# One stage instead of three: merge, the context's norm and its first queries

## The reference, cut to what matters

```python
merged = (g_a * (y_rw @ w_out_rwkv) + g_b * (y_cv @ w_out_conv) + g_c * (y_at @ w_out_attn))   # gates: sigmoids
x = x + gate1 * (merged @ w_o)
x = x + gate2 * peer_ffn(modulate(x, shift2, scale2), lp)      # modulate: rms_norm(x) * (1 + scale) + shift

# peer_ffn, per token and head (8 heads):
q = hx @ wq                                  # two halves of 64
s = q . sub_keys                             # 2 x 128 scores
sv, si = top_k(s, 16); comb = all 16 x 16 sums; fv, fi = top_k(comb, 16)
idx = e1 * 128 + e2                          # 16 of 16384 experts
out = sum_k softmax(fv)_k * gelu(u[idx_k] . hx) * v[idx_k]
```

## Time and profile before

| | |
|---|---|
| time, median of 3 runs | 5859.38 us (5856.72 to 5862.47) |
| the profiled execution's own time | 5852.54 us |
| its span | 5850.8 us |
| PE busy (matmul) | 4989.0 us, 85% |
| DVE / ACT / POOL busy | 3891.0 / 1440.8 / 1538.1 us |
| gathers of the expert stage (line 2108) | 1280, 640 a layer; their queue takes 56.9% of 16 engines' span |
| granted PE clock, mean | 0.948 of full speed |

### The profile page before, as it was taken

How to read it: one execution, slowest core, us unless ns; L and a number is a source line. 1 busy time by engine, 2 the same in 40 slices (tenths; PEclk the granted TensorE clock), 3 DMA queues, 4 the chain that set the end, 5 groups by cost and what they waited for, 6 DMA issues and landing times. The chain is left out here.

```text
span 5850.8 us, 72994 instructions
## 1 busy us (share of the span) xinstructions
PE 4989.0 (85%) x27348; PEld 2721.9 (47%) x27348; DVE 3891.0 (67%) x8901; ACT 1440.8 (25%) x3620; POOL 1538.1 (26%) x1408
## 2 busy tenths in 40 slices
PE   7988899978888888888789888999788888888887
PEld 4445588644333433333245455885433334333332
DVE  3556666537777777777645566665477777777776
ACT  1123211212222222222211232112122222322222
POOL 0100000004444444444301000000044444445443
PEclk9999899989999999999989998999899999999999
DMA  3213510549999999999932235105499999999999
GB/s 137 72 74 128 214 52 33 204 168 421 420 406 421 406 421 411 422 407 420 386 120 71 74 143 199 55 31 218 174 421 420 407 420 408 421 403 422 412 421 384
DMA packets 306824, 1644.51 MB, mean 281 GB/s; under 512 B 34696, under 2 KB 48264, under 8 KB 140832
## 3 DMA queue, kind: packets, MB, share of 16 engines
q0 software_dynamic: 193504, 1370.70, 56.9%
q1 hardware_dynamic: 112960, 269.08, 12.5%
HBM read 1575.84 MB, written 63.82 MB: 280 GB/s over the span
## 5 line engine op out<-in xcount | busy, mean ns | idle before, releaser
L2175 PE MATMUL psum<-peer_rows,peer_diagonal 128*128 128x512 f32 x5120 | 2512.6, 625 | 540.2 <-ACT peer_diagonal L2237 538.5
L2108 POOL DMA_INDIRECT peer_rows<-in_peer_rows,look_up_index x1280 | 1468.9, 1148 | 3008.9 <-PE psum L2175 1685.2
L2318 DVE CUSTOM_DVE_ANT_0 peer_rows<-peer_rows,h_rows 128x1024 f32<-128x1024 f32 x1280 | 1553.2, 1225 | 519.5 <-DMA peer_rows<-in_peer_rows,look_up_index 505.8
L2175 PEld LDWEIGHTS psum<-peer_rows,peer_diagonal 128*128 128x128 f32 x5120 | 937.3, 198 | 1575.9 <-issue 835.1
L2231 ACT ACTIVATE peer_active<-peer_dots 128x2 f32<-128x2 f32 (+1 forms) x642 | 130.8, 204 | 2058.3 <-DVE peer_dots L2318 2058.1
L2237 ACT ACTIVATE peer_diagonal<-ident_sb,peer_weight 128x128 f32<-128x128 f32 x1280 | 444.5, 394 | 145.4 <-DVE peer_weight L2271 143.2
L2122 PEld LDWEIGHTS psum<-h_sb,query_weights 128*128 128x128 f32 x1184 | 235.9, 199 | 304.4 <-issue 304.4
L481 PE MATMUL psum<-in_weights,h_sb 128*128 128x512 f32 (+1 forms) x800 | 309.9, 549 | 0.0
L1016 PE MATMUL psum<-h_sb,rw_in_gate_weights 128*128 128x512 f32 (+1 forms) x768 | 215.0, 441 | 29.2 <-DMA rw_in_gate_weights<-in_w_gate 29.2
L2271 DVE TENSOR_TENSOR peer_weight<-peer_active,peer_share 128x2 f32<-128x2 f32 (+1 forms) x642 | 104.0, 162 | 201.5 <-ACT peer_active L2231 201.5
L2122 PE MATMUL psum<-h_sb,query_weights 128*128 128x128 f32 x1184 | 235.8, 282 | 0.0
(11 more groups left out here) (361 smaller groups left out, 5878.4 us busy)
## 6 DMA issues: line engine op xcount, KB each, us to landing
rw_out_mod_weights<-in_w_mod SPq DMA_DIRECT2D x16, 2048.0 KB
in_weights<-in_w_in SPq DMA_DIRECT2D x12, 2048.0 KB, 8.6
peer_rows<-in_peer_rows,look_up_index POOLq DMA_INDIRECT x1280
modulation_weights<-in_w_mod SPq DMA_DIRECT2D x8, 2048.0 KB
scratch_rw_scratch<-rw_in_direction SPq DMA_DIRECT2D x20, 768.0 KB, 6.4
wkv_own<-scratch_rw_scratch SPq DMA_DIRECT2D x20, 768.0 KB, 6.5
rw_in_gate_weights<-in_w_gate POOLq DMA_DIRECT2D x24, 512.0 KB, 7.1
scratch_rw_scratch<-rw_in_z SPq DMA_DIRECT2D x10, 1024.0 KB, 5.9
```

The costliest lines, as they stand in the source:

```text
L2108: nc.gpsimd.indirect_dma_start(rows[spot][:, :], None, t.dram["peer_rows"], bass.IndirectOffsetOnAxis(ap=index[j % 4][:, k:k + 1], axis=0) ...
L2175: last = nc.tensor.matmul(t.bank[2 * (i % 2) + c], diagonal[k % DIAGONALS][:, :], rows[spot][:, D + c * 512:D + (c + 1) * 512], start=(j = ...
L2318: v.tensor_tensor_reduce(rows[spot][:, 0:D], rows[spot][:, 0:D], h[:, :], 1.0, 0.0, ALU.mult, ALU.add, dots[b][:, k:k + 1]).then_inc(s["do ...
```

## The change

The three stages merge, norm2 and peer_query become one, `context_stage`.

- The units run in the order context 0-1, latents 0-1, context 2-7, latents 2-7, over three PSUM banks instead of eight.
- PE projects the context after the first eleven units. The five latents' units left stand between the steps of the context's norm and queries, in an order written out by hand, and DVE's gating of them likewise.
- The sum of squares moves from ACT to DVE (`tensor_tensor_reduce`).
- The keys' load waits for the residual. SP's other loads keep their order.
- DVE does the whole search of head 0 with the gating of the last unit between `combine` and `number_experts`, and copies the scores of heads 1 and 2 after it; the two share banks with those of head 0, so PE computes scores 1 and 2 only when the scores before them have been copied.
- The stage has 29 semaphores; peer_query had 9.
- `t.h_rows`, `t.scores` and the look-up tiles go to the right side of SBUF. `normed`, `product` and `queries` lie in `t.y_conv` and `t.y_attn`, which have been read by then.
- `norm_stage` is left with its use in front of the branches; there it does the same as before.

The diff, cut to its core (what `scan`, `combine`, `number_experts`, the matmuls and the gating do is unchanged):

```diff
+def context_stage(nc, t, s, before, layer):
+
+    BANKS = 3
+    FIRST = 2
+    CONTEXT_MERGED = KD + FIRST
...
+        norm_sum, norm_root, norm_inverse = (sbuf(n, 1) for n in ("norm_sum", "norm_root", "norm_inverse"))
+        unused, unread = (y[:, :, :].rearrange("p j n -> p (j n)") for y in (t.y_conv, t.y_attn))
+        normed, product = unused[:, 0:D], unused[:, D:D + LAT]
+        queries = unread[:, 0:QUERIES_AHEAD * CTX].rearrange("p (h n) -> p h n", h=QUERIES_AHEAD)
...
+        units = [(i, g) for lo, hi in ((0, FIRST), (FIRST, KD)) for g in range(2) for i in range(lo, hi)]
+        parts = ((0, FIRST), (FIRST, KD))
+        weights_loaded, gates_loaded = (s["weights_loaded0"], s["weights_loaded1"]), (s["gates_loaded0"], s["gates_loaded1"])
+        last_banks, turned_banks, score_banks = t.bank[4:6], t.bank[6:8], t.bank[6:8]
+        query_banks = (t.bank[4], t.bank[5], t.bank[3])
 
...
             sp.dma_start(t.find.iota[:, :], t.dram["iota"].partition_broadcast(P)).then_inc(s["iota_loaded"], 16)
+            sp.wait_ge(s["residual"], 4)
+            sp.dma_start(t.key_rows, t.dram["peer_keys"][layer, :, :, :].rearrange("p h n -> p (h n)")).then_inc(s["keys_loaded"], 16)
...
+            def branch(n):
+                (i, g), (lo, m) = units[n], GROUPS[units[n][1]]
+                if g == 0 and i in (0, FIRST):
+                    pe.wait_ge(weights_loaded[i // FIRST], 16)
+                if n >= BANKS:
+                    pe.wait_ge(s["gated"], n - BANKS + 1)
...
+            def project():
+                pe.wait_ge(s["added"], CONTEXT_MERGED)
+                pe.wait_ge(s["last_loaded"], 32)
...
+            def turn_normed():
+                pe.wait_ge(s["normed"], 1)
...
             def query(h):
-                if h >= 2:
-                    pe.wait_ge(s["query_copied"], h - 1)
+                if h == 0:
+                    pe.wait_ge(s["query_loaded"], 32)
+                    pe.wait_ge(s["vector_wrote"], 1)
+                    pe.wait_ge(s["scalar_wrote"], 1)
...
             def score(h):
                 pe.wait_ge(s["query_copied"], h + 1)
-                if h >= 2:
-                    pe.wait_ge(s["scores_copied"], 2 * (h - 1))
+                if h:
+                    pe.wait_ge(s["scores_copied"], 2 * h)
+                else:
+                    pe.wait_ge(s["keys_loaded"], 16)
...
+            def turn_rows():
+                pe.wait_ge(s["query_copied"], 2)
...
+            for n in range(CONTEXT_MERGED + 1):
+                branch(n)
+            project()
+            branch(CONTEXT_MERGED + 1)
+            branch(CONTEXT_MERGED + 2)
+            turn_normed()
+            branch(CONTEXT_MERGED + 3)
             query(0)
+            branch(CONTEXT_MERGED + 4)
+            score(0)
             query(1)
...
             query(2)
+            turn_rows()
+            branch(CONTEXT_MERGED + 5)
             score(1)
             score(2)
...
+            act.wait_ge(s["averaged"], 1)
+            nc.scalar.activation(norm_root[:, :], norm_sum[:, :], ACT.Sqrt).then_inc(s["root"], 1)
+            act.wait_ge(s["normed_turned"], 2)
...
+            def gate(n):
+                (i, g), (lo, m) = units[n], GROUPS[units[n][1]]
+                if g == 0 and i in (0, FIRST):
+                    dve.wait_ge(s["sigmoid"], i // FIRST + 1)
+                dve.wait_ge(s["product"], n + 1)
+                v.tensor_tensor(product[:, 0:m], gates[:, i, lo:lo + m], t.bank[n % BANKS][:, 0:m], ALU.mult).then_inc(s["gated"], 1)
+                dve.wait_ge(s["gated"], n + 1)
+                v.tensor_tensor(t.h[:, i, lo:lo + m], t.h[:, i, lo:lo + m], product[:, 0:m], ALU.add).then_inc(s["added"], 1)
...
+            def update():
+                for c in range(2):
+                    cols = slice(c * 512, (c + 1) * 512)
+                    dve.wait_ge(s["projected"], c + 1)
+                    v.tensor_tensor(product[:, :], last_banks[c], t.gate_rows[:, 0, 0, cols], ALU.mult).then_inc(s["residual"], 1)
...
+            def average():
+                done.step(v.tensor_tensor_reduce(normed, t.x[:, 0, :], t.x[:, 0, :], 1.0, 0.0, ALU.mult, ALU.add, norm_sum[:, 0:1]))
+                v.tensor_scalar(norm_sum[:, :], norm_sum[:, :], 1.0 / D, RMS_EPS, ALU.mult, ALU.add).then_inc(s["averaged"], 1)
+
+            def normalise():
+                dve.wait_ge(s["root"], 1)
+                done.step(v.reciprocal(norm_inverse[:, :], norm_root[:, :]))
+                v.tensor_scalar(normed, t.x[:, 0, :], norm_inverse[:, 0:1], None, ALU.mult).then_inc(s["normed"], 1)
+
+            def modulate():
+                dve.wait_ge(s["normed_turned"], 1)
+                for k in range(4):
+                    last = v.tensor_scalar(t.h[:, k, 0:CTX], turned_banks[0][:, k * P:(k + 1) * P], t.mod[:, 4 * KD + k, 0:1], t.mod[:, 3 * KD + k, 0:1],
+                                           ALU.mult, ALU.add)
+                last.then_inc(s["vector_wrote"], 1)
 
             def copy_scores(h):
                 for c in range(2):
                     dve.wait_ge(s["scored"], 2 * h + c + 1)
-                    nc.vector.tensor_copy(t.scores[h % 2][:, c, :], score_bank[2 * (h % 2) + c][:, 0:KEYS]).then_inc(s["scores_copied"], 1)
-
+                    v.tensor_copy(t.scores[h % 2][:, c, :], score_banks[c][:, 0:KEYS]).then_inc(s["scores_copied"], 1)
+
...
+            for n in range(CONTEXT_MERGED + 1):
+                gate(n)
+            update()
+            average()
+            gate(CONTEXT_MERGED + 1)
+            normalise()
+            gate(CONTEXT_MERGED + 2)
+            modulate()
+            gate(CONTEXT_MERGED + 3)
+            gate(CONTEXT_MERGED + 4)
+            searches = Steps(dve, s["search"])
             copy_scores(0)
             dve.wait_ge(s["scores_copied"], 2)
-            t.find.scan(nc.vector, done, 0, 0)
+            t.find.scan(v, searches, 0, 0)
+            t.find.scan(v, searches, 0, 1)
+            t.find.combine(v, searches, 0)
+            gate(CONTEXT_MERGED + 5)
+            dve.wait_ge(s["iota_loaded"], 16)
+            t.find.number_experts(v, searches, 0, s["looked_up"])
             copy_scores(1)
-            t.find.scan(nc.vector, done, 0, 1)
             copy_scores(2)
-            t.find.combine(nc.vector, done, 0)
-            dve.wait_ge(s["iota_loaded"], 16)
-            t.find.number_experts(nc.vector, done, 0, s["looked_up"])
             dve.wait_ge(s["scores_copied"], 2 * QUERIES_AHEAD)
             dve.wait_ge(s["looked_up"], 1)
 
-        @block.scalar
-        def _(act):
-            def copy_query(h):
-                act.wait_ge(s["query"], h + 1)
-                nc.scalar.copy(queries[:, h, :], query_bank[h % 2][:, 0:CTX]).then_inc(s["query_copied"], 1)
-
-            copy_query(0)
-            copy_query(1)
-            for half in range(2):
-                act.wait_ge(s["turned"], half + 1)
-                nc.scalar.copy(t.h_rows[:, half * 512:(half + 1) * 512], t.bank[half]).then_inc(s["row_copied"], 1)
-            copy_query(2)
-            act.wait_ge(s["row_copied"], 2)
-
-
-PEER_QUERY = ("iota_loaded", "vector", "looked_up", "row_copied", "scores_copied", "turned", "query_copied", "query", "scored")
+
+CONTEXT = ("weights_loaded0", "weights_loaded1", "gates_loaded0", "gates_loaded1", "last_loaded", "query_loaded", "keys_loaded", "iota_loaded", "gated", "product",
+           "added", "residual", "projected", "sigmoid", "averaged", "root", "normed", "normed_turned", "vector_wrote", "scalar_wrote", "query", "query_copied",
+           "scored", "scores_copied", "turned", "row_copied", "vector", "search", "looked_up")
...
-          ("merge", MERGE), ("norm2", NORM), ("peer_query", PEER_QUERY), ("peer", PEER))
+          ("context", CONTEXT), ("peer", PEER))
...
-        t.out_weights = after.enter_context(nc.sbuf_tensor("last_weights", [P, KD, D], F32, side="right"))
-        t.query_weights = after.enter_context(nc.sbuf_tensor("query_weights", [P, KD, D], F32, side="right"))
-        merge_stage(nc, t, stages["merge"], stages["rwkv_output"], layer)
-    with ExitStack() as held:
+        def kept(name, *shape, dtype=F32):
+            return after.enter_context(nc.sbuf_tensor(name, [P, *shape], dtype, side="right"))
+
+        t.out_weights, t.query_weights = kept("last_weights", KD, D), kept("query_weights", KD, D)
         t.key_rows = t.gate_rows[:, 0, 0, :]
-        t.h_rows = held.enter_context(nc.sbuf_tensor("h_rows", [P, D], F32))
-        t.scores = [held.enter_context(nc.sbuf_tensor(f"peer_scores{b}", [P, 2, KEYS], F32)) for b in range(2)]
-        t.find = LookUp(t, lambda name, *shape, dtype=F32: held.enter_context(nc.sbuf_tensor("look_up_" + name, [P, *shape], dtype)))
-        norm_stage(nc, t, stages["norm2"], stages["merge"], 3, layer)
-        peer_query_stage(nc, t, stages["peer_query"], stages["norm2"])
-        peer_stage(nc, t, stages["peer"], stages["peer_query"], layer)
+        t.h_rows = kept("h_rows", D)
```

(52 more changed lines are left out.)

147 lines of the change are left out of this document (45 added, 102 removed).

## The result

| | before | after |
|---|---|---|
| time, median (lowest to highest) | 5859.96 us (5856.72 to 5862.47, 4 runs) | 5787.90 us (5783.55 to 5790.92, 4 runs) |
| ratio, 95% interval | | 0.9875 (0.9863 to 0.9887) |
| the profiled execution's own time, span | 5852.54, 5850.8 us | 5783.55, 5781.6 us |
| PE busy | 4989.0 us | 4963.6 us |
| first gather behind SP's first load of the merge, layer 1 / 2 | 90.34 / 89.98 us | 76.67 / 77.49 us |

The kernel is 72 us faster; 26.7 us were forecast, and the range ended at 5823. The two profiled executions are 69.0 us apart, and the last two lines of the table hold nearly all of it: 13.7 + 12.5 = 26.2 us from the merged stage, and 19.2 + 23.2 = 42.4 us from the gather streams, which the prediction had taken as untouched.

A forecast was written before the change was run, and what follows sets the result against it. The gather stream at 416 GB/s bounds most of the span; a latency chain delays its start in each layer. Gains of 13.5 and 13.2 us, 26.7 in all, off the 5859.38 median give 5832.7 us, range 5823 to 5842.

The forecast's parts named there:

- Its own sum: Merged stage, both layers: 14.9 us less 1.4 for clears gives 13.5 in layer 1, 13.2 in layer 2, 26.7 in all.
- The change touches nothing inside it: Expert stage: its gather stream stays as it was; only the moment when it begins can move, once per layer.
- then 416 GB/s: Expert stage, sign of being right: after the first gather at 1281.4 the stream runs at its old rate, 416 GB/s.
- the signs of being wrong: PE gaps ahead of transposes or query, projection after 1233, last score copy after 1281, expert stage longer by over 3 us.
- Rival (3): Expert stage: gathers slower because the ring moves in SBUF; at 1.5% slower 5881 us; chance 0.04.
- the wait ahead of the context blocks: Merged stage, before the projection: PE idles 3.0 us from 1221.6 until the sigmoid and gating free a bank.
- Rival (2): PE's clock falls in the 3.0 us wait and stays low until the projection is done: 5859 or so; chance 0.03.
- Both ends that the prediction gave: PE after the 3.0 us wait: full clock, nothing lost; or fallen clock, 1.9 us lost, 0.9 per layer net.
- a load behind the mean: ACT's table load in the norm: if behind the mean, PE loses 0.1 to 0.2 us per layer by the skill's page.
- The clears: Head of the expert stage: 20 more semaphore clears on GpSimd delay the first gather by 1.4 us, bounds 0 to 1.5.
- Rival (1): Merged stage: chain steps just miss PE and wait behind latents' blocks; gain 18 to 19 us, 5841; chance 0.12.
- Rival (4): Merged stage gains more, latents' blocks off the chain and sigmoid earlier; 35 us, 5824; chance 0.05.

The follow-up runs named there:

- e1: Kernel before the change, with 384 unused bytes ahead of the expert stage's ring so that it starts at byte 92672, a 256-byte multiple: 5819.94 us, ratio 0.9937.
- e4: Changed kernel with the gather ring shifted by 256 bytes of padding, so still on a 256-byte boundary: 5783.07 us, ratio 0.9874.
- g1: Changed kernel with clears behind sixteen gathers, second head's score copies ahead of the numbering, and plain loads' tiles on 256-byte boundaries: 5777.16 us, ratio 0.9859.
- f1: Changed kernel with GpSimd's 29 semaphore clears moved behind the expert stage's first sixteen gathers: 5783.03 us, ratio 0.9867.

## Why the prediction was wrong

Its own sum held, 26.2 us measured for 26.7. But it was the sum of little more than a third of the effect.

| step (layer 1, prediction's time base) | forecast | measured |
|---|---|---|
| PE starts | 1208.35 | 1208.35 |
| PE waits for the big sigmoid | from 1221.6, 3.0 us | from 1222.33, 1.88 us |
| projection starts, held by `w_o` | 1231.65 | 1231.32, `w_o` waited for 0.73 us |
| transposes of the norm | 1252.25 | 1252.00 |
| first query | 1256.55 | 1256.31 |
| numbering starts | 1272.2 | 1272.06 |
| stage ends | 1277.6 | 1277.50 |
| first gather | 1281.4 | 1281.20 |
| gain up to the first gather, layer 1 + 2 | 13.5 + 13.2 | 13.67 + 12.49 |

- **The step that failed**: "The change touches nothing inside it", and with it "then 416 GB/s". The change moved the ring onto the grid; the stream went at 421 to 422 GB/s and gave 42.4 us, a term that the sum had at nothing. e1 gets 39 us by padding alone. Even the signs of being wrong named only a longer expert stage.
- **Rival (3)** had the right object, the ring's place in SBUF, and the wrong evidence. It was dismissed because the rate is flat whichever ring place is filled. But the places are 8192 bytes apart, a multiple of 256, so all eight were equally off the grid and their flat rate could say nothing. Nor does show a rate by place: it is one mean over 400 us, in which every place is filled some twenty times. It was also priced on one side only: that a ring which lay badly could come to lie well was not considered. The addresses could be worked out from the allocations before any run.
- **The section of the Trainium skill** cited above (DMA: Bandwidth & Descriptors, How a descriptor splits into AXI transactions) is the one that bears most on this change, and the prediction did not weigh it.
- **What the stage is worth in time** is read from kernels with equally placed rings. Off the grid: four of the changed kernels (5827.21 to 5839.12) against the kernel before, timed beside each, 19.7, 19.7, 26.8 and 31.8 us, mean 24.5. On it: e4 against e1, timed side by side, 36.9 us. 26.7 lies among them; the time does not fix it any closer.
- **Layer 2** gained 12.49 us where 13.2 were forecast. Its part of the gates landed later: the big sigmoid started 16.88 us behind SP's first load, in place of 15.85 in layer 1, and `w_o` was waited for 0.75 us there too. From the projection's start to the first gather the layers agree, 49.88 and 49.65 us.
- **Clock**: the wait ahead of the context blocks cost nothing in the changed kernel, though it was 3.02 us long in layer 2 (row below). In 19 of the 20 layers of the ten kernels with this order the next 32 records took 6.38 us, behind waits of 1.19 to 3.02 us. In g1's layer 2 2.61 us of waiting did cost 1.65 us. **Rival (2)**, a clock that stays low until the projection is done, did not occur in any. Both ends that the prediction gave occur, then, and the length of the wait alone does not decide which.
- **The table load** went out as soon as the sigmoid was done, 24.5 us ahead of the root, and cost nothing, so the case of a load behind the mean did not arise.
- **The clears**: 1.4 us forecast for 20 more. From the last score copy to the first gather are 3.70 us, where 2.34 lay between the search's end and the gather before: 1.36. f1 shows that they are serial.
- **Rival (1)**, near-misses on PE: none missed. **Rival (4)** had the right side but no mechanism for it, and ended at 35 us, about half of what was measured.

The wait of layer 2 in the timeline of the changed kernel; its 32 records take the 6.38 us of full clock:

```profile
4110.76 6.38 PE L1930 MATMUL psum<-y_rw,merge_out_weights 128*128 128x128 f32 x32 [3.02 <-DVE y_conv L2026]
```

What stays open: why a start off the grid costs 4 to 5 ns of some 312 for each 8 KB packet, rather than 1/32 of it; whether transactions are the reason at all; why the streams differ by up to 7 us among the kernels off the grid; and why the times of those with the merged stage differ by 12.

## What to carry to other kernels

When an edit moves allocations, write down the start address of every tile that a saturated DMA stream fills, before and after, as part of the diff; "its code is unchanged" doesn't mean that it runs unchanged. Put such tiles on 256-byte boundaries: a line of padding was worth as much here as a reordered stage (39 us against 20 to 37). To move independent PE work into the waits of a chain paid twice here, in the time filled and in the clock that it keeps up, and the way to price it is the chain's own timeline.

## What the runs showed of the hardware

- The SBUF start of gathered 8 KB rows matters at 256-byte grain: the five kernels off the grid moved 413 to 417 GB/s in the two mid-stream stretches, those on it 420 to 424. The cost was the same for 32, 64, 128 and 224 bytes off.
- Plain loads with 2048-byte rows gained from the same alignment: 89.4 to 89.6 ns a packet in place of 90.6 to 91.4, and SP's issue of `peer_wq` 9.96 to 10.00 us in place of 10.51 to 10.55.
- One semaphore clear on POOL takes 0.07 us of its time, though its record says 44 ns, and 29 clears ahead of the first gather delayed it by 2.15 us in layer 1 (f1), all of their time.
